# A four-mixer network on one core: the first pair of an attention block projected without the norm's row factor

## The chip, the cores and the metric

One core of a Trainium2 chip runs the whole program. The metric is the device time of one execution in microseconds (us), lower is better. TensorE (PE) multiplies, PEld is its weight load, VectorE (DVE) and ScalarE (ACT) work elementwise, GpSimd (POOL) and the SyncE queue (SP) do the rest. The three runs shown of the kernel before have a median of 911.96 us.

## The reference

Four layers follow one another on a sequence of 256 positions with 1024 features: a gated delta rule mixer, an attention block ("the middle block" here, the reference's `moba_mixer`; with 256 positions it is plain causal attention within one block), a norm, a retention mixer and a chunked attention mixer. What matters for the change is the middle block's entry:

```python
def rms_norm(x, g):
    xf = x.astype(jnp.float32)
    y = xf * lax.rsqrt(jnp.mean(xf * xf, axis=-1, keepdims=True) + EPS)
    return (y * g.astype(jnp.float32)).astype(x.dtype)
...
    kv = rms_norm(x, kv_norm_g) @ w_kv
...
    x = x + moba_mixer(rms_norm(x, b_norm_g[j]), b_w_in[j], b_w_out[j], kb, vb, k_mean, rel_bias)
...
    proj = hn @ w_in
    q = proj[..., :B_W].reshape(bsz, s, B_HEADS, B_DH)
    z = proj[..., B_W:]
    o = moba_attention(q, kb, vb, k_mean, rel_bias)
    return (o * jax.nn.silu(z)).astype(hn.dtype) @ w_out
```

The factor `rsqrt(mean(x*x))` is one number for each position. It can be multiplied to x before the product with `w_in` or to the product's result.

## The kernel before

Everything is kept transposed: features on the 128 partitions, positions on the free axis. x is 8 tiles of 128 x 256. Each product is a "job" of 1024 x 256 weights: 8 tiles k, two output halves, and three matmuls for each, as every fp32 operand is split into a high part (rounded to fp32r) and a low part, and high-high, high-low and low-high are summed. So a job is 48 matmuls of 128 x 128 by 256 columns. Jobs alternate between two PSUM banks; `bank_free` counts when a bank's reader is done.

Weights stream in chunks of 1 MB, one for a job in this part of the program. SP issues chunk c after DVE has split chunk c - 3 (line 342). A chunk is split in two halves ("units"): ACT writes the high part `whi` (`high`, line 854, the instruction on line 863), DVE the low part `wlo` (`low`, line 1218, line 1234). Four units of each are held, and the high part of a unit waits for TensorE to be done with the unit four before it. Job J's chunk is J; in `attend` the engines split chunk J + 1 under the name of job J (`split_c` on ACT, `lows` on DVE).

Each engine's order is written out by hand, and it is strict. The part around the change:

- Jobs 16 to 19 (`JOB_OUT_A`) project the first mixer's output. DVE's `add_x` (line 1462) adds each job's bank to two tiles of x (line 1473); ACT's `square_x` (line 895) squares them (line 904).
- `x_sums(1)` (line 776): 8 fp32 products with ones sum the squares over the partitions. ACT's `rsqrt` (Ln on line 882, Exp on line 884) makes the row factor of it, after an explicit load of its function table (line 852) and the split of chunk 21.
- DVE multiplies x by the row factor into `hf` (line 1549, four instructions). ACT makes high parts of `hf` times the gain for two operands (line 1145): `b_norm` into `ohi` tiles 8 to 15, then `kv_norm` into `hhi`. DVE makes the low parts (`lo_of`, line 1546).
- The middle block (`attend`, jobs 20 to 35): four pairs of heads, each with four jobs, q (J), z (J + 1), k (J + 2) and v (J + 3). q and z read the b_norm operand, k and v the kv_norm operand. For pair i the scores (fp32 products of `qn` and `kn`) come behind job J + 3, `turn(i)`, the transposes of the softmax on line 733, behind job J + 5, and `mix(i)` behind J + 6. ACT copies q, k and v out of PSUM and applies Silu to z.
- Beside this, DVE sums the conditioning matrices ("ADA", `pair_sums`, lines 1312 to 1319): pair n is summed behind the split of chunk `ADA_AT[n]`, the ring for the next one is loaded by SP three chunks later, and TensorE's `ada` follows job `ADA_AT[n]`.

Of the kernel before, what the change touches and what calls it, by code (L numbers as in the profile page):

```python
# [18 lines left out]
KT = D // P  # L19
# [3 lines left out]
F32 = mybir.dt.float32  # L23
# [36 lines left out]
    return [JOB_OUT_D + 4 + 2 * (job - JOB_OUT_D) + h for h in range(2)]  # L60


ADA_AT = [10, 11, 12, 13, 14, 15, 23, 26, 29, 32, 35, 43, 46, 48, 51, 53, 56, 58, 61, 63, 78, 82, 86, 90]


def laid_at(c):
# [8 lines left out]
def two_blocks(nc, x_in, wts, ada_w, cols_in, const_in, lmask_in, w_ab, rel_b, rel_d, dtab, pos, out,  # L75
               scr_b, scr_d):
    ctx = ExitStack()
    with ctx:
# [172 lines left out]
        rs_ok_sem = sem("rs_ok")  # L251
        hf_ok_sem = sem("hf_ok")
        hh_ok_sem = sem("hh_ok")
        h_ok_sem = sem("h_ok")
        dve_own_sem = sem("dve_own")
        ab_ok_sem = sem("ab_ok")
# [182 lines left out]
        def _(pe):  # L439
# [9 lines left out]
                else:  # L449
                    pe.wait_ge(bank_free[J % 2], max(J // 2 - 6, 0))  # L450

            def job(J, form, hi, lo, ready=None, split=None, at={}, heads=2):

                bank = v2(pj[J % 2])
                bank_empty(J)
                cs = chunks_of(J)
                for n, c in enumerate(cs):
                    for half in range(2):
                        unit = 2 * c + half
                        pe.wait_ge(lo_ok_sem, unit + 1)  # L460
                        for kk in range(4):
                            k = 4 * half + kk
                            kx = 8 * n + k
                            if kx in at:
                                at[kx]()
                            if split is not None and kx % heads == 0:
                                pe.wait_ge(o_split_sem, split + kx // heads + 1)
                            if ready is not None and n == 0:
                                pe.wait_ge(h_ok_sem, ready + k + 1)
                            for t in range(2):  # L470
                                w = slice(t * P, t * P + P)
                                for a, (ws, hs) in enumerate(((whi, hi), (whi, lo), (wlo, hi))):
                                    first = n == 0 and k == 0 and t == 0 and a == 0
                                    last = n == len(cs) - 1 and k == KT - 1 and a == 2
                                    if form == "T":
                                        m = mm(bank[:, t, :], ws[:, unit % UNITS, kk, w], hs[:, kx, :], first, last)
                                    else:
                                        m = mm(bank[:, t, :], hs[:, kx, w], ws[:, unit % UNITS, kk, :], first, last)
                        m.then_inc(w_units_sem, 1)
# [242 lines left out]
            def attend(J0, pairs, soft0, o0, h_q, h_kv, normed, ready, extra):  # L722
# [28 lines left out]
                for i in range(pairs):  # L751
                    J = J0 + 4 * i
                    h_1, h_2 = (h_kv, h_q) if normed else (h_q, h_kv)
                    job(J, "T", *h_q, ready=ready[0] if i == 0 else None)
                    extra(J)
                    job(J + 1, "T", *h_1)
                    extra(J + 1)
                    if i:
                        turn(i - 1)
                    if normed:  # L760
                        sums(lambda t: sqb[:, 0:2, :], 1, 512, qk_sq_sem, lambda t: 4 + 2 * i + 1)
                    job(J + 2, "T", *h_2, ready=ready[1] if i == 0 and not normed else None)
                    extra(J + 2)
                    if i:
                        mix(i - 1)
                    if normed:
                        sums(lambda t: sqb[:, 2:4, :], 1, 512, qk_sq_sem, lambda t: 4 + 2 * i + 2)
                    job(J + 3, "S", *h_kv)
                    extra(J + 3)
                    if normed:  # L770
                        scores(i, soft0, lambda: pe.wait_ge(qk_ok_sem, 2 * i + 2))
                    else:
                        scores(i, soft0, lambda: banks_copied(J))
                return lambda: turn(pairs - 1), lambda: mix(pairs - 1)

            x_sums(1)

            turn_last, mix_last = attend(JOB_B, 4, 0, 4, (ohi[:, 8:16, :], olo[:, 8:16, :]), (hhi, hlo), False, (8, 16), ada_after)
            for J in range(JOB_OUT_B, JOB_C):
                if J == JOB_OUT_B:  # L780
                    job(J, "T", ohi, olo, split=4, at={4: turn_last, 6: mix_last})
# [53 lines left out]
                ada_after(J)  # L835
            x_sums(3)

            turn_last, mix_last = attend(JOB_D, 8, 4, 12, (hhi, hlo), (hhi, hlo), True, (32, 32), ada_after)
            for J in range(JOB_OUT_D, N_JOBS):
                if J == JOB_OUT_D:  # L840
                    job(J, "T", ohi, olo, split=12, at={8: turn_last, 12: mix_last})
# [5 lines left out]
        def _(act):  # L847
# [47 lines left out]
            def square_x(J0, gain=None):  # L895

                for n in range(4):
                    J = J0 + n
                    for c in chunks_of(J):
                        if n or c > chunks_of(J0)[0] or J0 == JOB_OUT_A:  # L900
                            high(c + 1)
                    bank_taken(act, J)
                    if gain is None:
                        act.activation(xsq[:, 2 * n:2 * n + 2, :], x[:, 2 * n:2 * n + 2, :], ACT.Square).then_inc(sq_ok_sem, 1)
                    else:
                        for t in (2 * n, 2 * n + 1):
                            m = act.activation(xsq[:, t, :], x[:, t, :], ACT.Square, scale=gain(t))
                        m.then_inc(sq_ok_sem, 1)
# [153 lines left out]
            def attend(J0, pairs, soft0, v0, normed):  # L1062
# [18 lines left out]
                for i in range(pairs):  # L1081
# [4 lines left out]
                    if i:  # L1086
                        if normed:
                            ln_exp_set()
                        soft(i - 1)
                    if not normed:  # L1090
                        act.wait_ge(w_units_sem, 2 * chunks_of(J)[-1] + 2)
                        act.wait_ge(s_ok_sem, 2 * (soft0 + i))
                        act.activation(qn[:, :, :], bank(J), ACT.Copy).then_inc(bank_free[J % 2], 1)
                        if i:
                            split_c(J + 1)
                        act.wait_ge(w_units_sem, 2 * chunks_of(J + 1)[-1] + 2)
                        act.activation(zs[:, 2 * (i % 2):2 * (i % 2) + 2, :], bank(J + 1), ACT.Silu).then_inc(bank_free[(J + 1) % 2], 1)
                        if i == 2:
                            act.wait_ge(fin_rope_sem, 2)
                            act.activation(sint, tr1, ACT.Sin)  # L1100
                            act.activation(cost, tr2, ACT.Sin).then_inc(fin_rope_sem, 1)
                        if i:
                            turned(i - 1)
                        split_c(J + 2)
                        split_c(J + 3)
                        act.wait_ge(w_units_sem, 2 * chunks_of(J + 2)[-1] + 2)
                        act.activation(kn[:, :, :], bank(J + 2), ACT.Copy).then_inc(bank_free[J % 2], 1)
                        act.wait_ge(w_units_sem, 2 * chunks_of(J + 3)[-1] + 2)
                        act.wait_ge(o_ok_sem, v0 + i)
                        act.activation(vs[:, :, 0:256], bank(J + 3), ACT.Copy).then_inc(bank_free[(J + 3) % 2], 1)  # L1110
                        continue
# [27 lines left out]
            ln_exp_set()  # L1139
            high(JOB_B + 1)  # L1140
            rsqrt(rsb[:, 0, :], S, 1.0 / D)
            for dst, gain in ((ohi[:, 8:16, :], "b_norm"), (hhi, "kv_norm")):
                for t in range(KT):
                    act.wait_ge(hf_ok_sem, 8 + t // 2 + 1)
                    act.activation(dst[:, t, :], hf[:, t, :], ACT.Copy, scale=col(gain, t)).then_inc(hh_ok_sem, 1)
            high(JOB_B + 2)
            attend(JOB_B, 4, 0, 4, False)

# [59 lines left out]
        def _(dve):  # L1208
# [253 lines left out]
            def add_x(J0, gate=None, before_last=None):  # L1462

                for n in range(4):
# [6 lines left out]
                    sums_done(J)  # L1471
                    if gate is None:
                        dve.tensor_tensor(x[:, 2 * n:2 * n + 2, :], bank(J), x[:, 2 * n:2 * n + 2, :], ALU.add).then_inc(bank_free[J % 2], 1)
                    else:
                        for t in range(2):
                            k = 2 * n + t
# [3 lines left out]
            def attend(J0, pairs, soft0, bias, normed):  # L1480
# [31 lines left out]
                for i in range(pairs):  # L1512
# [6 lines left out]
                        scale_p(i - 1)  # L1519
                    if normed or i:  # L1520
                        lows(J + 1)
                    lows(J + 2)
                    if normed:
                        next_rs()
                        dve.wait_ge(s_ok_sem, 2 * (soft0 + i))
# [17 lines left out]
            def lo_of(prep, t, gain, hi, lo):  # L1543

                dve.wait_ge(hh_ok_sem, 8 * prep + t + 1)
                dve.scalar_tensor_tensor(out=lo[:, t, :], in0=hf[:, t, :], scalar=col(gain, t), in1=hi[:, t, :].bitcast(F32), op0=ALU.mult, op1=ALU.subtract).then_inc(h_ok_sem, 1)

            for n in range(4):
                dve.tensor_tensor(hf[:, 2 * n:2 * n + 2, :], x[:, 2 * n:2 * n + 2, :], wide(rsb[:, 0, :], 2), ALU.mult).then_inc(hf_ok_sem, 1)
                if n:  # L1550
                    for t in (2 * n - 2, 2 * n - 1):
                        lo_of(1, t, "b_norm", ohi[:, 8:16, :], olo[:, 8:16, :])
            for t in (6, 7):
                lo_of(1, t, "b_norm", ohi[:, 8:16, :], olo[:, 8:16, :])
            for t in range(KT):
                lo_of(2, t, "kv_norm", hhi, hlo)
            low(JOB_B + 2)
            dve.wait_ge(bias_ok_sem, 128)
            attend(JOB_B, 4, 0, A(bias_at, 8, 384), False)
            def scaled_gain(l):  # L1560
# [211 lines left out]
```

## Time and profile before

| | |
|---|---|
| median of the three runs | 911.96 us (909.32 to 914.17) |
| the profiled execution | 909.5 us, span 907.6 us |
| mean granted clock of TensorE | 0.981 |
| TensorE matmul busy | 858.5 us, 95% |
| DVE busy | 580.2 us, 64% |
| ACT busy | 481.2 us, 53% |
| jobs 16 to 19 | about 210 to 236 us |
| middle block and its output projection | about 244 to 382 us |

Times in all rows are from the start of the span. The last add of jobs 16 to 19 is at 236 us. A matmul's row is its own duration, which overlaps with the next one's; the spacing of two starts is what one costs in a stream. The granted clock is 1.00 at 2.4 GHz and 0.50 at 1.2 GHz. A merged row carries a count (x16).

### The profile page before, as it was taken

How to read it: one execution, taken by the hardware profiler on the slowest of the kernel's cores; microseconds unless marked ns; L12 is line 12 of the kernel's file. 1: busy time of each engine (PE TensorE's matmuls, PEld its weight loads, DVE VectorE, ACT ScalarE, POOL GpSimd, SP SyncE). 2: the span in 40 equal slices, each digit the busy share in tenths (PEclk: the TensorE clock that was granted, in tenths of full speed). 3: DMA queues.
4: the chain of work that ended last, by engine and by line, in shares of the span. 5: the costliest groups of instructions: out<-in, count | busy, mean ns of one | idle time of the engine just before them, and what ended most of it. 6: DMA issues, size and time to landing. Idle time of an engine off the chain costs nothing.

```text
span 907.6 us, 16161 instructions
## 1 busy us (share of the span) xinstructions
PE 858.5 (95%) x6742; PEld 830.6 (92%) x6742; DVE 580.2 (64%) x1025; ACT 481.2 (53%) x740; POOL 33.5 (4%) x57
## 2 busy tenths in 40 slices
PE   5999999999899998989979998898999999999998
PEld 4899999998799998989979998798999999999998
DVE  4886875637657667477766786446476666656652
ACT  5754554345655654555443433345676576666741
POOL 2100500002000000000000000200000000000000
PEclk9999999999899999999999999899999999999999
DMA  6463654333746465426646464496354464434350
GB/s 264 147 217 109 108 186 148 134 99 93 244 175 219 165 232 187 139 94 229 236 139 215 157 235 182 124 257 223 140 197 172 148 224 143 147 133 153 129 207 24
DMA packets 26487, 153.69 MB, mean 169 GB/s; under 512 B 2848, under 2 KB 3376, under 8 KB 12080
## 3 DMA queue, kind: packets, MB, share of 16 engines
q1 hardware_dynamic: 24432, 146.37, 46.7%
q0 software_dynamic: 1984, 6.31, 3.8%
q8 instruction: 53, 0.87, 0.4%
q14 instruction: 18, 0.15, 0.1%
HBM read 150.04 MB, written 2.62 MB: 168 GB/s over the span
## 4 chain that ended last, share of the span: by engine, by line
PE 86%; DVE 9%; ACT 3%; issue 1%; DMA 1%; SPq 0%; DVEq 0%; ACTq 0%
PE ps L443 83%; DVE wlo L1234 2%; PE ps L637 1%; DVE olo L1279 1%; ACT whi L863 1%; PE ps L733 1%; ACT L852 1%; DVE arena L1594 1%; DVE arena L1590 1%; DMA raw<-weights 1%; DVE ohi L1277 1%; DVE ada_ring L1315 0%; DVE arena L1301 0%; ACT arena L882 0%; DVE early L1266 0%
## 5 line engine op out<-in xcount | busy, mean ns | idle before, releaser
L1234 DVE TENSOR_TENSOR wlo<-raw,whi 128x1024 fp32r<-128x1024 f32 x224 | 265.3, 1222 | 176.9 <-ACT whi L863 176.9
L443 PE MATMUL ps<-hhi,whi 128*128 128x256 f32 x960 | 280.7, 292 | 18.5 <-DVE wlo L1234 7.9
L443 PE MATMUL ps<-hlo,whi 128*128 128x256 f32 x960 | 273.4, 285 | 0.0
L443 PE MATMUL ps<-hhi,wlo 128*128 128x256 f32 x960 | 273.3, 285 | 0.0
L863 ACT ACTIVATE whi<-raw 128x1024 fp32r<-128x1024 f32 x224 | 225.9, 1052 | 82.8 <-PE ps L443 61.2
L443 PEld LDWEIGHTS ps<-hhi,whi 128*128 128x128 f32 x960 | 185.8, 194 | 22.9 <-issue 22.1
L443 PEld LDWEIGHTS ps<-hlo,whi 128*128 128x128 f32 x960 | 186.0, 194 | 2.0 <-issue 1.9
L443 PEld LDWEIGHTS ps<-hhi,wlo 128*128 128x128 f32 x960 | 185.8, 194 | 0.0
L443 PE MATMUL ps<-ohi,whi 128*128 128x256 f32 x512 | 149.8, 293 | 12.5 <-DVE olo L1279 7.9
L443 PE MATMUL ps<-olo,whi 128*128 128x256 f32 x512 | 147.5, 288 | 0.0
L443 PE MATMUL ps<-ohi,wlo 128*128 128x256 f32 x512 | 147.3, 288 | 0.0
L443 PEld LDWEIGHTS ps<-ohi,whi 128*128 128x128 f32 x512 | 101.0, 197 | 14.0 <-issue 9.9
L443 PE MATMUL ps<-arena 128*128 128x128 f32 (+2 forms) x656 | 101.0, 302 | 3.0 <-DVE olo L1279 3.0
L443 PEld LDWEIGHTS ps<-arena 128*128 128x128 f32 x656 | 92.2, 195 | 10.0 <-issue 5.5
L443 PEld LDWEIGHTS ps<-olo,whi 128*128 128x128 f32 x512 | 101.0, 197 | 0.3 <-issue 0.2
L443 PEld LDWEIGHTS ps<-ohi,wlo 128*128 128x128 f32 x512 | 100.8, 197 | 0.0
L443 PE MATMUL ps<-whi,hhi 128*128 128x256 f32 x320 | 94.2, 294 | 0.0
L443 PE MATMUL ps<-wlo,hhi 128*128 128x256 f32 x320 | 90.5, 283 | 0.0
L443 PE MATMUL ps<-whi,hlo 128*128 128x256 f32 x320 | 90.5, 283 | 0.0
L443 PEld LDWEIGHTS ps<-whi,hhi 128*128 128x128 f32 x320 | 61.4, 192 | 1.9 <-issue 1.9
L443 PEld LDWEIGHTS ps<-whi,hlo 128*128 128x128 f32 x320 | 61.3, 192 | 1.9 <-issue 1.9
L443 PEld LDWEIGHTS ps<-wlo,hhi 128*128 128x128 f32 x320 | 61.3, 192 | 0.0
(194 smaller groups left out, 867.6 us busy)
## 6 DMA issues: line engine op xcount, KB each, us to landing
raw<-weights SPq DMA_DIRECT2D x112, 1024.0 KB, 5.0
ada_ring<-ada SPq DMA_DIRECT2D x24, 1024.0 KB, 5.1
arena<-bias_rows_d POOLq DMA_DIRECT2D x4, 512.0 KB, 14.1
x<-x_t SPq DMA_DIRECT2D x2, 512.0 KB, 4.5
bias_rows_d<-early POOLq DMA_DIRECT2D x1, 1024.0 KB, 12.4
arena<-bias_rows_b POOLq DMA_DIRECT2D x4, 256.0 KB, 7.3
arena<-bias_rows_d POOLq DMA_DIRECT2D x4, 256.0 KB, 16.2
out_t<-x SPq DMA_DIRECT2D x4, 256.0 KB, 2.2
```

Source lines behind the costliest of these rows:

```text
L443: return pe.matmul(o, l, r, start=start, stop=stop, skip_group_check=skip)
L637: m = pe.transpose(b[:, m4 * P:m4 * P + P], tt[:, 4 * g + m4, :], ident)
L733: m = pe.transpose(turned_bank(hh, soft0)[:, a * P:a * P + P], ts[:, hh, c0:c0 + P], ident)
L852: act.add_instruction(mybir.InstLoadActFuncSet(name=nc.get_next_instruction_name(), act_func_set_id=6, ins=[], outs=[]))
L863: act.activation(whi[:, unit % UNITS, :, :], raw[:, c % RAW, 4 * half:4 * half + 4, :], ACT.Copy).then_inc(hi_ok_sem, 1)
L1234: dve.tensor_tensor(wlo[:, unit % UNITS, :, :], raw[:, c % RAW, 4 * half:4 * half + 4, :], whi[:, unit % UNITS, :, :].bitcast(F32), ALU.su ...
L1277: own(dve.tensor_copy(ohi[:, r, :], src))
L1279: return dve.tensor_tensor(olo[:, r, :], src, ohi[:, r, :].bitcast(F32), ALU.subtract)
L1590: own(dve.tensor_tensor(of[:, :, :], v2(ps[3 + b]), wide(rsb[:, 0, :], 2), ALU.mult))
L1594: own(dve.scalar_tensor_tensor(out=of[:, t, :], in0=of[:, t, :], scalar=col("ret_gn", 4 * h + k), in1=zs_c[:, 4 * (h % 2) + k, :], op0=ALU ...
```

## The change

For the first pair alone, q and z (jobs 20 and 21) are projected from x times the gain, without the row factor, and DVE multiplies both results by the row factor when it takes them out of PSUM. In detail:

- While jobs 16 to 19 run, ACT makes the high parts of x times `b_norm` into `hhi` (8 instructions, ahead of each square), and DVE the low parts into `hlo` (8, one job behind, the last four behind the last add). TensorE waits for these low parts on `xg_lo_sem`.
- `x_sums(1)` moves from ahead of job 20 to between its k = 3 and k = 4.
- After the row factor, DVE and ACT make the `kv_norm` operand, now into `ohi`/`olo` tiles 8 to 15, and only later, behind the splits of chunk 23, the `b_norm` operand for pairs 1 to 3, now into `hhi`/`hlo`.
- DVE's order becomes: `hf` and kv low parts 0 to 5, q of job 20 times the factor (instead of ACT's copy), first half of chunk 22, kv low parts 6 and 7, second half, z of job 21 times the factor, chunk 23, eight low parts of `b_norm`. ACT applies Silu to the scaled z in place.
- Four ADA places move: 23, 26, 29, 32 become 25, 28, 30, 33.

```diff
-ADA_AT = [10, 11, 12, 13, 14, 15, 23, 26, 29, 32, 35, ...
+ADA_AT = [10, 11, 12, 13, 14, 15, 25, 28, 30, 33, 35, ...
...
+                    elif i == 0:
+                        job(J, "T", *h_q, ready=0, ready_sem=xg_lo_sem, at={4: lambda: x_sums(1)})
+                    else:
+                        job(J, "T", *h_q, ready=16 if i == 1 else None)
...
-            x_sums(1)
...
                     bank_taken(act, J)
+                    if J0 == JOB_OUT_A:
+                        for t in (2 * n, 2 * n + 1):
+                            act.activation(hhi[:, t, :], x[:, t, :], ACT.Copy, scale=col("b_norm", t)).then_inc(xg_hi_sem, 1)
...
-                    if not normed:
+                    if not normed and i == 0:
+                        act.wait_ge(z0_scaled_sem, 1)
+                        act.activation(zs[:, 0:2, :], zs[:, 0:2, :], ACT.Silu).then_inc(bank_free[(J + 1) % 2], 1)
+                        split_c(J + 2)
+                        for t in range(KT):
+                            act.activation(hhi[:, t, :], hf[:, t, :], ACT.Copy, scale=col("b_norm", t)).then_inc(hh_ok_sem, 1)
+                        split_c(J + 3)
+                    elif not normed:
...
+                        if J0 == JOB_OUT_A:
+                            for m in (n - 1, n) if n == 3 else (n - 1,):
+                                for t in range(2 * m, 2 * m + 2) if m >= 0 else ():
+                                    dve.wait_ge(xg_hi_sem, t + 1)
+                                    dve.wait_ge(bank_free[(JOB_OUT_A + m) % 2], (JOB_OUT_A + m) // 2 - 5)
+                                    dve.scalar_tensor_tensor(out=hlo[:, t, :], in0=x[:, t, :], scalar=col("b_norm", t), in1=hhi[:, t, :].bitcast(F32), op0=ALU.mult, op1=ALU.subtract).then_inc(xg_lo_sem, 1)
...
+            sums_done(JOB_B)
+            dve.tensor_tensor(qn[:, :, :], bank(JOB_B), wide(rsb[:, 0, :], 2), ALU.mult).then_inc(bank_free[JOB_B % 2], 1)
+            low(JOB_B + 2, range(1))
+            kv_lo(6)
+            kv_lo(7)
+            low(JOB_B + 2, range(1, 2))
+            sums_done(JOB_B + 1)
+            dve.tensor_tensor(zs[:, 0:2, :], bank(JOB_B + 1), wide(rsb[:, 0, :], 2), ALU.mult).then_inc(z0_scaled_sem, 1)
+            dve.wait_ge(z0_scaled_sem, 1)
+            low(JOB_B + 3)
             for t in range(KT):
-                lo_of(2, t, "kv_norm", hhi, hlo)
-            low(JOB_B + 2)
+                lo_of(2, t, "b_norm", hhi, hlo)
```

## Rows read from the trace of the kernel before

**Rows 1.** The page, section 1: busy time, share, instructions by engine.

```profile
PE 858.5 (95%) x6742; PEld 830.6 (92%) x6742; DVE 580.2 (64%) x1025; ACT 481.2 (53%) x740; POOL 33.5 (4%) x57
```

**Rows 2.** TensorE's waits, 251 to 382 us: total us, times, longest.

```profile
PE ps L443 <- DVE olo L1279: 2.0, 1, 2.0
PE ps L733 <- issue: 0.7, 1, 0.7
```

**Rows 3.** Chain of waits, 234 to 260 us: start, us, what.

```profile
236.22 0.70 DVE x L1473
...
237.59 1.28 ACT L852
...
238.89 1.06 ACT whi L863
...
239.98 2.36 DVE wlo L1234 x2
```

**Rows 4.** Timeline of TensorE, 235 to 260 us: start, us, instruction, [idle before <-releaser].

```profile
236.02 3.62 PE L443 MATMUL ps<-arena,ones 128*128 128x256 f32 x16
244.15 0.55 PE L443 MATMUL ps<-ohi,whi 128*128 128x256 f32 x1 [4.51 <-DVE olo L1546]
...
250.05 0.36 PE L443 MATMUL ps<-ohi,whi 128*128 128x256 f32 x1
...
258.40 0.28 PE L443 MATMUL ps<-hhi,whi 128*128 128x256 f32 x1
258.52 0.28 PE L443 MATMUL ps<-hlo,whi 128*128 128x256 f32 x1
```

**Rows 5.** TensorE by stretch (busy, PEclk, DMA share, GB/s) and in the timeline.

```profile
244.00:250.00 6.00, 5.85 (x27) 0.50 0.39 153
...
362.00:368.00 6.00, 6.00 (x40) 0.72 0.12 51
...
521.00:527.00 6.00, 6.00 (x51) 1.00 0.70 201
...
361.54 0.39 PE L443 MATMUL ps<-ohi,whi 128*128 128x256 f32 x1 [1.97 <-DVE olo L1279]
...
520.36 0.35 PE L443 MATMUL ps<-hhi,whi 128*128 128x256 f32 x1 [1.94 <-DVE wlo L1234]
```

**Rows 6.** Timeline of ACT, 236 to 260 us.

```profile
236.95 0.63 ACT L904 ACTIVATE arena<-x 128x512 f32<-128x512 f32 x1 [3.23 <-DVE x L1473]
...
240.80 0.45 ACT L882 ACTIVATE arena<-ps,epsc 128x256 f32<-128x256 f32 x1
...
246.43 0.91 ACT L1145 ACTIVATE ohi<-arena,columns 128x256 fp32r<-128x256 f32 x2 [0.49 <-DVE arena L1549]
...
254.45 1.28 ACT L1097 ACT_TABLE_LOAD   x1
258.60 0.60 ACT L1097 ACTIVATE arena<-ps 128x512 f32<-128x512 f32 x1 [2.87 <-PE ps L443]
```

**Rows 7.** Timeline of DVE, 232 to 253 us; line 1590 by form (busy, mean ns).

```profile
232.80 2.36 DVE L1234 TENSOR_TENSOR wlo<-raw,whi 128x1024 fp32r<-128x1024 f32 x2 [1.58 <-ACT whi L863]
...
242.25 1.29 DVE L1549 TENSOR_TENSOR arena<-x,arena 128x512 f32<-128x512 f32 x2
...
246.31 1.67 DVE L1546 SCALAR_TENSOR_TENSOR olo<-arena,columns,ohi 128x256 fp32r<-128x256 f32 x4
...
251.52 1.23 DVE L1234 TENSOR_TENSOR wlo<-raw,whi 128x1024 fp32r<-128x1024 f32 x1 [0.37 <-ACT whi L863]
...
L1590 DVE TENSOR_TENSOR arena<-ps,arena 128x512 f32<-128x512 f32 x5 | 3.4, 686 | 0.1
```

**Rows 8.** The page, section 6: DMA issues, count, KB each, us to landing.

```profile
ada_ring<-ada SPq DMA_DIRECT2D x24, 1024.0 KB, 5.1
```

**Rows 9.** DVE's timeline and the chain of waits near chunk 30's split.

```profile
309.36 2.36 DVE L1234 TENSOR_TENSOR wlo<-raw,whi 128x1024 fp32r<-128x1024 f32 x2 [0.68 <-ACT whi L863]
...
310.41 0.71 PE ps L733 x6
```

More of the change, by code:

```diff
@@ L60, in chunks_of @@
     return [JOB_OUT_D + 4 + 2 * (job - JOB_OUT_D) + h for h in range(2)]
-ADA_AT = [10, 11, 12, 13, 14, 15, 23, 26, 29, 32, 35, 43, 46, 48, 51, 53, 56, 58, 61, 63, 78, 82, 86, 90]
+ADA_AT = [10, 11, 12, 13, 14, 15, 25, 28, 30, 33, 35, 43, 46, 48, 51, 53, 56, 58, 61, 63, 78, 82, 86, 90]
 def laid_at(c):
@@ L253, in two_blocks @@
         hh_ok_sem = sem("hh_ok")
+        xg_hi_sem = sem("xg_hi")
+        xg_lo_sem = sem("xg_lo")
+        z0_scaled_sem = sem("z0_scaled")
         h_ok_sem = sem("h_ok")
@@ L450, in bank_empty, with job @@
                     pe.wait_ge(bank_free[J % 2], max(J // 2 - 6, 0))
-            def job(J, form, hi, lo, ready=None, split=None, at={}, heads=2):
+            def job(J, form, hi, lo, ready=None, split=None, at={}, heads=2, ready_sem=h_ok_sem):
                 bank = v2(pj[J % 2])
@@ L468, in job @@
                             if ready is not None and n == 0:
-                                pe.wait_ge(h_ok_sem, ready + k + 1)
+                                pe.wait_ge(ready_sem, ready + k + 1)
                             for t in range(2):
@@ L753, in attend @@
                     h_1, h_2 = (h_kv, h_q) if normed else (h_q, h_kv)
-                    job(J, "T", *h_q, ready=ready[0] if i == 0 else None)
+                    if normed:
+                        job(J, "T", *h_q, ready=ready if i == 0 else None)
+                    elif i == 0:
+                        job(J, "T", *h_q, ready=0, ready_sem=xg_lo_sem, at={4: lambda: x_sums(1)})
+                    else:
+                        job(J, "T", *h_q, ready=16 if i == 1 else None)
                     extra(J)
@@ L761, in attend @@
                         sums(lambda t: sqb[:, 0:2, :], 1, 512, qk_sq_sem, lambda t: 4 + 2 * i + 1)
-                    job(J + 2, "T", *h_2, ready=ready[1] if i == 0 and not normed else None)
+                    job(J + 2, "T", *h_2, ready=ready if i == 0 and not normed else None)
                     extra(J + 2)
@@ L774, in attend @@
                 return lambda: turn(pairs - 1), lambda: mix(pairs - 1)
-            x_sums(1)
-            turn_last, mix_last = attend(JOB_B, 4, 0, 4, (ohi[:, 8:16, :], olo[:, 8:16, :]), (hhi, hlo), False, (8, 16), ada_after)
+            turn_last, mix_last = attend(JOB_B, 4, 0, 4, (hhi, hlo), (ohi[:, 8:16, :], olo[:, 8:16, :]), False, 8, ada_after)
             for J in range(JOB_OUT_B, JOB_C):
@@ L836, in _ @@
             x_sums(3)
-            turn_last, mix_last = attend(JOB_D, 8, 4, 12, (hhi, hlo), (hhi, hlo), True, (32, 32), ada_after)
+            turn_last, mix_last = attend(JOB_D, 8, 4, 12, (hhi, hlo), (hhi, hlo), True, 32, ada_after)
             for J in range(JOB_OUT_D, N_JOBS):
@@ L1093, in attend @@
                         act.activation(qn[:, :, :], bank(J), ACT.Copy).then_inc(bank_free[J % 2], 1)
-                        if i:
-                            split_c(J + 1)
+                        split_c(J + 1)
                         act.wait_ge(w_units_sem, 2 * chunks_of(J + 1)[-1] + 2)
@@ L1101, in attend @@
                             act.activation(cost, tr2, ACT.Sin).then_inc(fin_rope_sem, 1)
-                        if i:
-                            turned(i - 1)
+                        turned(i - 1)
                         split_c(J + 2)
                         split_c(J + 3)
+                    if not normed:
                         act.wait_ge(w_units_sem, 2 * chunks_of(J + 2)[-1] + 2)
@@ L1141, in _ @@
             rsqrt(rsb[:, 0, :], S, 1.0 / D)
[L1142 to L1145, printed above, removed]
+            for t in range(KT):
+                act.wait_ge(hf_ok_sem, 8 + t // 2 + 1)
+                act.activation(ohi[:, 8 + t, :], hf[:, t, :], ACT.Copy, scale=col("kv_norm", t)).then_inc(hh_ok_sem, 1)
             high(JOB_B + 2)
@@ L1521, in attend @@
                         lows(J + 1)
-                    lows(J + 2)
+                        lows(J + 2)
                     if normed:
@@ L1546, in lo_of @@
                 dve.scalar_tensor_tensor(out=lo[:, t, :], in0=hf[:, t, :], scalar=col(gain, t), in1=hi[:, t, :].bitcast(F32), op0=ALU.mult, op1=ALU.subtract).then_inc(h_ok_sem, 1)
+            kv_lo = lambda t: lo_of(1, t, "kv_norm", ohi[:, 8:16, :], olo[:, 8:16, :])
             for n in range(4):
@@ L1550, in _ @@
                 if n:
[L1551 to L1554, printed above, removed]
+                    kv_lo(2 * n - 2)
+                    kv_lo(2 * n - 1)
+            sums_done(JOB_B)
[8 more added lines that the diff above has]
+            low(JOB_B + 3)
             for t in range(KT):
-                lo_of(2, t, "kv_norm", hhi, hlo)
-            low(JOB_B + 2)
+                lo_of(2, t, "b_norm", hhi, hlo)
             dve.wait_ge(bias_ok_sem, 128)
```

## The prediction

> **What bounds the kernel now.** I read the page first: TensorE is busy 858.5 of 907.6 us, DVE and ACT far less [rows 1]. So time can only be won where TensorE stands still or runs at half its clock. The table of waits for the middle attention block says where that is not the case: from 251 us to 382 us TensorE waits for 2.7 us in all, for two causes [rows 2]. Whatever is won ahead of 251 us is therefore handed on, if the block is still fed in time.
>
> The chain of waits around the seam between the output projection (jobs 16 to 19) and the block (jobs 20 on) shows what is won there [rows 3]. The last add to x starts at 236.22, a table load at 237.59 (1.28 us), the split of chunk 21 on ACT at 238.89 and on DVE at 239.98 (2.36 us) and then the products with the row factor; job 20 starts at 244.15 [rows 4], released by a low part of b_norm's. TensorE's own list shows the same from its side [rows 4]: the sums of squares (8 fp32 products, 16 records) run from 236.02 for 3.62 us; then nothing for 4.51 us; then job 20 at 244.15, and job 22, the first to read the kv operand, at 258.40. Jobs 20 and 21 are 96 matmuls. They take 258.40 - 244.15 = 14.25 us; at the spacing of the full clock, 258.52 - 258.40 = 0.12 us, they would take 11.52. The missing 2.73 us lie in the first 28: they need 250.05 - 244.15 = 5.90 us, 0.21 each, and the granted clock from 244 to 250 is 0.50, that is 1.2 GHz, after TensorE had stood idle [rows 5].
>
> **The change part by part.**
>
> The old stretch from the start of the sums to the start of job 22 is 258.40 - 236.02 = 22.38 us [rows 4]. The new one holds half of job 20 (k 0 to 3, 24 matmuls, 2.88 us), the sums, the other half, and job 21. For the sums I take 3.5 us: 16 spacings of about 0.215, or with the drain 3.62 [rows 4]. If nothing waits: 2.88 + 3.5 + 2.88 + 5.76 = 15.0 us. The difference is 7.4 us: the idle 4.5, the half clock 2.7, and 0.2 of latency at the first matmul. Job 20 no longer needs the row factor, so what it does need must be ready by 236.0.
>
> Start of job 20: its operand is x times the gain, high part by ACT, low part by DVE. Tiles 0 to 3 are made beside jobs 17 to 19 and are long ready. Tiles 6 and 7 follow the last add, which ends at 236.9: ACT makes the high parts at about 0.45 each (2 in 0.91) [rows 6], DVE the four outstanding low parts at 0.42 each (4 in 1.67) [rows 7], done by 238.6. TensorE wants tile 4 only after the sums, at 242.4. Cover: nearly 4 us. The squares move 0.9 us later behind two high parts: 236.95 + 0.9 + 0.63 = 238.5. The sums start at 238.9 and take the last squares as their last two products. Cover again.
>
> Work added while jobs 16 to 19 run: 8 ACT instructions (3.6 us) and 8 DVE instructions (3.4 us). The high parts stand ahead of the splits of chunks 18 to 20, which move back by 0.9 us. Of chunk 20, DVE's low part started at 232.80 [rows 7]; now at 233.7, its first half done at 234.9, and job 20 wants it at 236.0. Chunks 18 and 19 have the same order and about the same spare time of 1 us. I cost it at nothing; without that cover it is 0.9 us once.
>
> The row factor: the sums now end at about 242.5 instead of 239.6. But ACT first splits chunk 21, from 239.8 (squares 238.5 plus the 1.28 table load) to 241.8; before, this pushed the Ln to 240.80 [rows 6]. Now Ln starts at 242.55, Exp ends at 243.45, and DVE starts the product x times the factor at 243.5 instead of 242.25 [rows 7], only 1.25 later.
>
> Then a queue on DVE decides. From the rows of before, shifted by 1.25: the four products and six low parts of the kv operand end at 248.4 (before, numbers 4 to 7 started at 246.31, four in 1.67 [rows 7]); q times the factor out of PSUM, 0.69 as the product of the same shape on line 1590 [rows 7], ends at 249.1; the split of chunk 22 waits for ACT (its eight kv high parts end at 248.6: before, the last two of the first operand started at 246.43 and took 0.91 [rows 6]; the first half of the chunk's high part follows at 249.6) and ends its first half at 250.8, at 1.23 a half [rows 7]. Job 22 wants it at 251.0. Slack 0.2. Two low parts and the second half end at 252.8, wanted at 253.9. Then z times the factor ends at 253.5, Silu at 254.1, the high part of chunk 23 at 255.1 and 256.1, its low part at 256.3 and 257.5; job 23 wants it at 256.8 and 259.7. Slack 0.5. The wait for job 21's end (251.0) in front of z's product costs nothing, as DVE comes there at 252.8. Behind that product are queued chunk 23's split and the eight low parts of b_norm; for these wait pair 1's jobs.
>
> The eight high and low parts of b_norm: ACT 256.0 to 259.3, DVE 257.5 to 260.8, then chunk 24 till 262.1 and 263.3. Job 24 starts at 262.6 plus the scores, 263.9. Slack 1.8. The keys' copy behind them on ACT ends at 262.0, wanted at 262.6. Nothing on the path, if the above holds.
>
> The q copy of ACT for the first pair goes (0.6), DVE gets two products (1.4). All that nets out away from TensorE.
>
> The moved ADA places (23, 26, 29, 32 to 25, 28, 30, 33): 8 DVE instructions and a sum, 3.5 us each, the same number; the ring's DMA is still issued three chunks later behind them on SP's queue, and at 5.1 us to landing [rows 8] the shortest distance, two chunks from 28 to 30, gives it over 10. What matters is that the sum of chunk 25 now stands in front of pair 0's scores. Before, chunk 29's stood so in front of pair 1's: there chunk 30's low part starts at 309.36, its first half ends at 310.6, and TensorE turned pair 1 at 310.41 for 0.71 us [rows 9] and went on without a wait [rows 2]. Slack 0.5. The same pattern now comes at chunk 25 and 33. I take it at 0.
>
> Sum: -7.4, with 0 for the feeds, whose bound is 0 to 1.5. Bound below: nothing here can win more than 7.4 except a luckier clock later.
>
> One rule weighed. The load of Silu's table stands in the trace right behind the q copy, at 254.45, while the Silu itself starts at 258.60 [rows 6]: it runs ahead of the wait. In the change it would then run at 250.5 to 251.8, ahead of the wait for z's product at 253.5, and cost nothing; behind the wait it would put 1.28 us into the link with slack 0.5, so 0.8 on the path. The Trainium skill (ScalarE: Activation LUTs, "What ACT_TABLE_LOAD costs") gives a switch 2.66 us, a drain being half of it. By it the load would still just fit ahead of the wait, and behind it cost an estimated 2.2. The rows show no such drain: the load at 237.59 takes 1.28 and the next ACT instruction starts at 238.89 [rows 3].
>
> **The rivals.**
>
> A, fed late: the slacks of 0.2 and 0.5 (and 0.5 at chunk 26) are smaller than what I can read from shifted rows. If each slips, TensorE waits 0.5 to 1 us at jobs 22, 23 or 26, 1.5 in all: gain 5.9, time 906.1. For it: everything passes through one DVE queue. Against: each term has a measured row.
>
> B, the clock takes it back later: TensorE's half-clock stretches behind later waits don't follow from the length of the wait alone. After 1.97 us of idle, at 361.54, the granted clock is 0.72 for six us; after 1.94 us, at 520.36, it is 1.00 [rows 5]. All later work moves by 7.4 us, so each stretch can come out otherwise, 1.7 us apiece at 0.72 (six us times 0.28). Two more such: +3.4, time 908.0. Two fewer: 901.2. The three times of before, 909.3 to 914.2, spread as much. The Trainium skill (TensorE: Matmul & The Clock Gate, "What's actually happening") says that the activity monitor's window is free-running and not tied to the kernel's start, which fits these two rows.
>
> C, slower: the ADA sums of 3.5 us stand in front of the scores at chunks 25 and 33, and their slack of 0.5 turns negative. Then TensorE waits for the softmax and for chunks 26 and 34, up to 3.5 us at each place, and falls to half clock, 2.7 each: 12.4 - 7.4 = +5.0, time 917.0. It decides from the point where chunk 26's first low half ends after pair 0's turn. Against it: the precedent of chunk 29 [rows 9].
>
> D, the change doesn't do what it says: job 20 still waits, say for the low parts of x, or the sums for the squares. The cover is 4 us; to lose it all, job 20 would have to wait for the table load and chunk 21 as before. Then only extra work is left: 912.
>
> **How the numbers follow.** The profiled execution took 909.5 us for a span of 907.6; less 7.4 that is 902.1 and 900.2. It is at the low end of the three runs shown, whose median is 911.96, so the forecast for the median is 911.96 - 7.4 = 904.6. Chances: the forecast 0.57, A 0.20, B 0.17 (half to each side), C 0.02, D 0.04. The range takes in A, B and the spread of the runs: 901 to 909. A measurement of this kernel can tell about 0.5% from no change, which is 4.6 us. Faster by more than that needs a gain above 4.6: the forecast 0.57, nearly all of A 0.19, half of B 0.09, together 0.85. Within it: D, the rest of B and A, 0.13. Slower: C, 0.02.
>
> **What would show it.** Right: between 236 and 262 us no idle row of TensorE above 0.5, a granted clock of 1.00 there, the sums' 16 records between two halves of job 20 near 239, job 22 at about 251.0, scores of pair 0 at about 262.6. Job 22 or 23 with idle time released by DVE's wlo is A. Half-clock stretches other than before behind 355 us are B. A wait at about 276 us is C. A first product of x and the row factor later than 244 would make the whole link late and the forecast wrong by that much.

## The result

The changed kernel takes 904.64 us (904.05 to 905.05, five runs) against 910.57 for the kernel before on the same chip (909.32 to 914.17, five runs). The medians differ by 5.9 us, 0.65%. The ratio of the runs on record is 0.9923, 95% interval 0.9907 to 0.9940: 0.8% faster, which is 5.5 to 8.5 us. Forecast were 904.6 us and a gain of 7.4, and both agree with this. The profiled execution of the changed kernel took 904.05 us, span 902.2; that of before 909.5 and 907.6.

The same work as in [rows 4], on TensorE's timeline of the changed kernel (line 446 is line 443 of before):

```profile
238.38 0.28 PE L446 MATMUL ps<-hhi,whi 128*128 128x256 f32 x1
...
241.26 3.61 PE L446 MATMUL ps<-arena,ones 128*128 128x256 f32 x16
244.52 0.47 PE L446 MATMUL ps<-hhi,whi 128*128 128x256 f32 x1
...
253.34 0.29 PE L446 MATMUL ps<-ohi,whi 128*128 128x256 f32 x1
```

Job 20 starts at 238.38, directly behind job 19, with tile 0 of x times the gain. Its first half ends at 241.26, the sums run for 3.61 us between the halves, and job 22, the first reader of the kv operand (now `ohi`), starts at 253.34. From the end of job 19 to job 22 it is 14.96 us; it was 22.38. The idle row of 4.51 us is gone, and by stretch the clock is whole:

```profile
238.00:244.00 6.00, 6.00 (x42) 5.69 (x41) 3.46 (x7) 4.67 (x6) 0.00 (x0) 1.00 0.81 325
244.00:250.00 6.00, 6.00 (x50) 5.90 (x49) 5.63 (x11) 3.57 (x9) 0.00 (x0) 1.00 0.53 179
250.00:256.00 6.00, 6.00 (x53) 6.00 (x52) 5.17 (x9) 4.35 (x6) 0.00 (x0) 1.00 0.01 4
```

(columns: stretch, us, then busy time and count of PE, PEld, DVE, ACT, POOL, granted clock, DMA share, GB/s). TensorE is busy all 18 us at a granted clock of 1.00, which is 2.4 GHz; before, 244 to 250 showed 0.50 [rows 5].

DVE's queue, which [rows 7] was the source for:

```profile
245.87 1.29 DVE L1570 TENSOR_TENSOR arena<-x,arena 128x512 f32<-128x512 f32 x2 [0.37 <-ACT arena L890]
...
250.74 0.68 DVE L1575 TENSOR_TENSOR arena<-ps,arena 128x512 f32<-128x512 f32 x1
251.95 1.23 DVE L1248 TENSOR_TENSOR wlo<-raw,whi 128x1024 fp32r<-128x1024 f32 x1 [0.53 <-ACT whi L869]
...
255.02 0.68 DVE L1581 TENSOR_TENSOR arena<-ps,arena 128x512 f32<-128x512 f32 x1
257.42 2.36 DVE L1248 TENSOR_TENSOR wlo<-raw,whi 128x1024 fp32r<-128x1024 f32 x2 [1.72 <-ACT whi L869]
259.70 3.26 DVE L1566 SCALAR_TENSOR_TENSOR hlo<-arena,columns,hhi 128x256 fp32r<-128x256 f32 x8
```

The first half of chunk 22's low part ends at 251.95 + 1.23 = 253.18, and job 22 reads it at 253.34: a slack of 0.16 us. (Where job 22 did wait for this half, in e4 and e8 below, it started 0.10 us after the end of the half, so some 0.06 us of it was to spare.) The row of 251.95 tells one thing more: DVE had stood idle 0.53 us for ACT's high part. And on ACT the table for Silu is loaded ahead of the wait for z:

```profile
252.89 1.28 ACT L1101 ACT_TABLE_LOAD   x1
255.74 0.63 ACT L1101 ACTIVATE arena<-arena 128x512 f32<-128x512 f32 x1 [1.57 <-DVE arena L1581]
```

But the whole stretch lies 2.36 us later in the span than before, although all work up to job 16 is the same. So I cut each profiled execution into three: up to the last add to x (its start), from there to the first pair's transposes (`turn(0)`), and the rest of the span. The add and the turn of the changed kernel:

```profile
238.58 0.69 DVE L1487 TENSOR_TENSOR x<-ps,x 128x512 f32<-128x512 f32 x1 [0.26 <-PE ps L446]
...
278.03 0.85 PE L736 MATMUL ps<-cst,arena 128*128 128x128 f32 x6
```

The names e1 to e8 are those of the experiments below; the last three columns are lengths in us.

| profiled execution | last add at | add to turn | rest | span |
|---|---|---|---|---|
| before | 236.22 | 46.96 | 624.4 | 907.6 |
| before once more (e7) | 236.50 | 46.96 | 624.4 | 907.9 |
| before with idle products in the wait (e2) | 239.03 | 44.31 | 623.1 | 906.4 |
| changed | 238.58 | 39.45 | 624.2 | 902.2 |
| changed once more (e6) | 240.04 | 39.46 | 628.5 | 908.0 |
| changed, sums ahead of job 20 (e3) | 238.42 | 39.46 | 624.3 | 902.2 |
| changed, ADA places back (e1) | 236.22 | 40.55 | 624.1 | 900.9 |
| changed, two products more (e4) | 238.85 | 40.03 | 627.3 | 906.2 |
| changed, four products more (e8) | 238.46 | 41.22 | 625.6 | 905.3 |
| changed, idle products in seven later waits (e5) | 236.52 | 39.46 | 616.1 | 892.1 |

The middle column is what the change acts on. It repeats to 0.01 us and falls from 46.96 to 39.45, by 7.51 us. The other two hold little of the change, and move by up to 4 us. Ahead of the last add stand the first products of x and the gain; TensorE's last wait ahead of it ends at 216.78 in the kernel before and at 219.13 in the changed one, 19.44 and 19.45 us ahead of the add, so they cost nothing. Behind the first turn stand three of the moved ADA places.

### The profile page after: what moved, and what is told of

Read it like the earlier page. It is cut to its first block, busy times and chain, and to the rows that moved or that the text cites. A ratio compares the mean times of both kernels' runs of the same rounds, so it can differ in the third digit from the quotient of the medians.

```text
span 902.2 us, 16186 instructions
## 1 busy us (share of the span) xinstructions
PE 857.1 (95%) x6742; PEld 828.9 (92%) x6742; DVE 584.0 (65%) x1035; ACT 483.5 (54%) x747; POOL 33.5 (4%) x57
## 4 chain that ended last, share of the span: by engine, by line
PE 86%; DVE 8%; ACT 3%; issue 1%; DMA 1%; SPq 0%; DVEq 0%; ACTq 0%
PE ps L446 84%; DVE wlo L1248 2%; PE ps L640 1%; DVE olo L1293 1%; PE ps L736 1%; ACT whi L869 1%; DVE arena L1622 1%; ACT L858 1%; DVE arena L1618 1%; DMA raw<-weights 1%; DVE ohi L1291 1%; DVE ada_ring L1329 0%; DVE arena L1315 0%; ACT arena L888 0%; DVE early L1280 0%
## 5 line engine op out<-in xcount | busy, mean ns | idle before, releaser
L446 PE MATMUL ps<-hhi,whi 128*128 128x256 f32 x1024 | 299.1, 292 | 18.8 <-DVE wlo L1248 7.9
L446 PE MATMUL ps<-hlo,whi 128*128 128x256 f32 x1024 | 291.2, 284 | 0.0
L446 PE MATMUL ps<-ohi,whi 128*128 128x256 f32 x448 | 130.2, 291 | 7.9 <-DVE olo L1293 7.9
L446 PE MATMUL ps<-olo,whi 128*128 128x256 f32 x448 | 128.2, 286 | 0.0
L446 PE MATMUL ps<-ohi,wlo 128*128 128x256 f32 x448 | 128.0, 286 | 0.0
L446 PE MATMUL ps<-whi,hhi 128*128 128x256 f32 x256 | 75.8, 296 | 0.0
L446 PE MATMUL ps<-wlo,hhi 128*128 128x256 f32 x256 | 72.4, 283 | 0.0
L446 PE MATMUL ps<-whi,hlo 128*128 128x256 f32 x256 | 72.4, 283 | 0.0
L1329 DVE SCALAR_TENSOR_TENSOR ada_ring<-ada_ring,sil 128x256 f32<-128x256 f32 x144 | 60.1, 488 | 0.0
L446 PE MATMUL ps<-arena,ones 128*128 128x256 f32 (+1 forms) x132 | 43.6, 461 | 8.5 <-DVE arena L1298 8.5
```

Of the source, the lines that this page charges most:

```text
L446: return pe.matmul(o, l, r, start=start, stop=stop, skip_group_check=skip)
L1329: own(dve.scalar_tensor_tensor(out=b, in0=b, scalar=sil[:, k:k + 1], in1=ring[:, :, k - 2, :], op0=ALU.mult, op1=ALU.add))
```

## The experiments

**What each part of the gain is.** e2 leaves the wait of before and takes only the half clock away:

```diff
             x_sums(1)
+            for _ in range(19):
+                mm(ps[3][:, :], ident_r[:, :], causal_r[:, :].unsqueeze(1).to_broadcast([P, 4, P]), True, True)
```

> The kernel before, with 19 products of 512 columns into an unused PSUM bank behind the sums of squares, whose results nobody reads; they fill the 4.5 us in which TensorE stands idle. It takes the half clock away and leaves the wait. My theory (the gain of 7.4 us is 4.7 of wait and 2.7 of half clock): granted clock 1.00 from 244 to 250 us, job 20 starts when it did, job 22 comes 2.7 us earlier, time 910.6 - 2.7 = 907.9. Rival: the clock falls for another reason (the change of operand, the cold stretch is due to the phase): still a stretch at 0.50, time 910 to 911.

Measured 908.99 us against 910.73 (12 and 23 runs), ratio 0.9984, 0.9968 to 1.0000. TensorE's timeline:

```profile
238.83 3.61 PE L443 MATMUL ps<-arena,ones 128*128 128x256 f32 x16
242.09 4.68 PE L443 MATMUL ps<-causal_r,ident_r 128*128 128x512 f32 x19
246.97 0.36 PE L443 MATMUL ps<-ohi,whi 128*128 128x256 f32 x1 [0.19 <-DVE olo L1548]
```

and the stretch behind it:

```profile
246.80:252.80 6.00, 5.83 (x49) 5.87 (x50) 6.00 (x16) 5.17 (x13) 0.00 (x0) 1.00 0.40 160
```

Job 20 starts 246.97 - 238.83 = 8.14 us behind the start of the sums, as before (244.15 - 236.02 = 8.13 [rows 4]): the wait is untouched. The clock behind it is 1.00, and the part from add to turn is 44.31 instead of 46.96, 2.65 us less. So of the 7.5 us, 2.7 are the half clock; what is left, 4.9, is the wait with its latency, by difference. The rival, that the clock would fall for another reason than the wait, is out for this place. The whole time fell by 1.7 and not by 2.7, to 908.99 and not to the 907.9 expected; the interval reaches to no change at all, so the time cannot carry the verdict. The stretch can.

**Whether the sums had to go inside job 20.** e3:

```diff
-                        job(J, "T", *h_q, ready=0, ready_sem=xg_lo_sem, at={4: lambda: x_sums(1)})
+                        job(J, "T", *h_q, ready=0, ready_sem=xg_lo_sem)
...
+            x_sums(1)
             turn_last, mix_last = attend(JOB_B, 4, 0, 4, (hhi, hlo), ...
```

> The changed kernel with the sums of squares ahead of job 20 again instead of between its halves. My theory: six of the eight sums need only older squares and take 2.6 us, by which time the last squares are just ready, so TensorE waits 0.0 to 0.3 us; the row factor comes 2.9 us earlier less ScalarE's split of chunk 21, which delays it; the stretch from job 19's end to job 22 stays 15.0 to 15.3 us and the time is 904.6 to 904.9. Rival: the place inside job 20 is what hides the squares and the table load; without it TensorE waits 1 us or more, 905.6 or later.

Measured 904.81 us (6 runs), ratio 0.9926 (0.9905 to 0.9946), the same as the changed kernel. Its timelines of TensorE and DVE:

```profile
238.22 3.61 PE L446 MATMUL ps<-arena,ones 128*128 128x256 f32 x16
241.48 0.47 PE L446 MATMUL ps<-hhi,whi 128*128 128x256 f32 x1
...
253.18 0.28 PE L446 MATMUL ps<-ohi,whi 128*128 128x256 f32 x1
```

```profile
242.97 2.36 DVE L1249 TENSOR_TENSOR wlo<-raw,whi 128x1024 fp32r<-128x1024 f32 x2 [2.29 <-ACT whi L870]
245.25 1.29 DVE L1571 TENSOR_TENSOR arena<-x,arena 128x512 f32<-128x512 f32 x2
...
251.32 1.23 DVE L1249 TENSOR_TENSOR wlo<-raw,whi 128x1024 fp32r<-128x1024 f32 x1 [0.53 <-ACT whi L870]
```

The stretch to job 22 is 253.18 - 238.22 = 14.96 us, the same to the hundredth. The sums run without a gap, so the last squares were in time. The place of the sums carries nothing of the gain. What it changes is slack: chunk 22's first half is now ready at 252.55, 0.63 us ahead of job 22 instead of 0.16. It is not the 2.9 us that the sums moved, as DVE is at chunk 21 until 245.3 whatever the row factor does.

**The slack at job 22.** e4 puts two more products ahead of q's on DVE, e8 four:

```diff
+            for to in (of, kn):
+                dve.tensor_tensor(to[:, :, :], bank(JOB_B), wide(rsb[:, 0, :], 2), ALU.mult)
             dve.tensor_tensor(qn[:, :, :], bank(JOB_B), wide(rsb[:, 0, :], 2), ALU.mult).then_inc(bank_free[JOB_B % 2], 1)
```

> The changed kernel with two more products of 0.69 us on VectorE ahead of q's (their results are not used), 1.4 us in the queue in front of chunk 22. My theory (the feed of job 22 has a slack of 0.2 us): job 22 starts 1.2 us late, released by wlo, the rest moves with it, time 905.8. Rival (VectorE has room, busy 65%): job 22 starts where it did, 904.6.

Measured 904.95 us (902.26 to 908.05, 6 runs), ratio 0.9929 (0.9904 to 0.9954): in the time nothing can be told. From add to turn it is 40.03, that is +0.58, about half of what I expected and not the rival's nothing. DVE and TensorE:

```profile
251.00 1.29 DVE L1576 TENSOR_TENSOR arena<-ps,arena 128x512 f32<-128x512 f32 x2
252.20 0.69 DVE L1577 TENSOR_TENSOR arena<-ps,arena 128x512 f32<-128x512 f32 x1
252.80 1.22 DVE L1248 TENSOR_TENSOR wlo<-raw,whi 128x1024 fp32r<-128x1024 f32 x1
```

```profile
254.12 0.36 PE L446 MATMUL ps<-ohi,whi 128*128 128x256 f32 x1 [0.35 <-issue]
```

The chunk's row has lost its idle time before it. Its half ends at 252.80 + 1.22 = 254.02, and job 22 starts at 254.12; the trace names no engine as its releaser ("issue"), the two times do. I had counted the slack on TensorE's side and left out that DVE itself was waiting for ACT there (249.1 against 249.6 in my own working). By the starts of the rows, two more products put q's back by 252.20 - 251.00 = 1.20 us; 0.53 were idle, 0.16 slack, and 0.51 is left to show, against 0.58 measured. With four this makes a forecast that can fail:

> The changed kernel with four more products of 0.69 us on VectorE ahead of q's instead of two (results unused). With two, job 22 came 0.6 us late and not 1.2: VectorE had stood idle 0.5 us for ScalarE's high part of chunk 22, and 0.2 us was slack. If that is so, two more cost their whole 1.3 us: from the last add to the first turn 39.45 + 0.6 + 1.3 = 41.3 to 41.4 us. Rival: TensorE makes it up later by shorter waits, as with two: 40.0 to 40.6.

Measured 41.22 us from add to turn, 1.19 more than with two, and an idle row of 1.53 ahead of job 22 (DVE first, then TensorE):

```profile
250.61 2.48 DVE L1576 TENSOR_TENSOR arena<-ps,arena 128x512 f32<-128x512 f32 x4
253.01 0.68 DVE L1577 TENSOR_TENSOR arena<-ps,arena 128x512 f32<-128x512 f32 x1
```

```profile
254.92 0.36 PE L446 MATMUL ps<-ohi,whi 128*128 128x256 f32 x1 [1.53 <-issue]
```

The one run took 907.23 us. Four products put q's back by 253.01 - 250.61 = 2.40 us; less 0.69 that is 1.71, and 1.77 was measured (41.22 - 39.45). The last two alone cost 1.20 us of DVE and made the stretch 1.19 us longer. Beyond the first 0.7 us, each us put ahead of chunk 22 on DVE is a us of the stretch, and the rival, that TensorE makes it up later, is out. DVE's busy share of 65% says nothing here.

**What the moved ADA places do.** e1 puts them back:

```diff
-ADA_AT = [10, 11, 12, 13, 14, 15, 25, 28, 30, 33, 35, ...
+ADA_AT = [10, 11, 12, 13, 14, 15, 23, 26, 29, 32, 35, ...
```

> The changed kernel with the four ADA places back at 23, 26, 29, 32. My theory: the sum of 3.5 us behind chunk 23 then stands on VectorE ahead of the eight low parts of b_norm and of chunk 24, whose first half would be ready about 1.4 us after job 24 could start. TensorE waits there for wlo or hlo, 1.0 to 1.5 us, and the time is 905.7 to 906.1 against 904.6 for the changed kernel. Rival: the sums find room anywhere, since VectorE is busy 65% of the span: no wait at job 24, 904.2 to 905.0.

Measured 907.3 us (902.75 to 911.45, 12 runs), ratio 0.9965, 0.9946 to 0.9984. DVE and TensorE:

```profile
257.86 2.46 DVE L1329 SCALAR_TENSOR_TENSOR ada_ring<-ada_ring,sil 128x256 f32<-128x256 f32 x6
260.36 0.43 DVE L1333 TENSOR_TENSOR ada_sum<-ada_ring 128x256 f32<-128x256 f32 x1
260.70 3.25 DVE L1566 SCALAR_TENSOR_TENSOR hlo<-arena,columns,hhi 128x256 fp32r<-128x256 f32 x8
263.87 4.62 DVE L1248 TENSOR_TENSOR wlo<-raw,whi 128x1024 fp32r<-128x1024 f32 x4
```

```profile
265.18 0.35 PE L446 MATMUL ps<-hhi,whi 128*128 128x256 f32 x1 [0.77 <-issue]
```

Job 24 waits 0.77 us for chunk 24 behind the sum, and the part from add to turn is 1.10 longer, as expected of the mechanism. The time was expected at 905.7 to 906.1 and missed that: the median of 907.3 is 2.5 us above that of e3, measured beside it, which is more than the mechanism. Whether the rest is the clock or something else, the one profiled execution can't say: it was the shortest of the twelve. So the moved places are part of the gain, 1.1 us of it shown.

**What the time outside the stretch hangs on.** Two kernels once more:

> The changed kernel once more, to pair with the next and to see whether the last add to x ahead of job 20 falls at 236.2 or at 238.4 to 239.0 us, where traces of kernels with the same work until then differ. If that is the state of the clock early in the program and not the change, it can fall at either; from the last add to the first turn 39.4 to 39.5 us in any case; time 904 to 905.5.

> The kernel before once more. From the last add to x to the first turn it took 47.0 us, of which 2.7 hang on a stretch at half clock. If that stretch can come out shorter, it is 45 to 47 us here; the last add at 236.2 or 238.4 to 239.0 us; time 909 to 912.

e6: 904.76 us (902.07 to 909.86, 6 runs), ratio 0.9945 (0.9923 to 0.9966); e7: 909.80 in one run. From add to turn 39.46 and 46.96: both repeat, and the half clock at job 20 did not come out shorter in e7. The last add fell at 240.04 and at 236.50; the former is later than either value that I had named. The granted clock of 72 to 78 us, where the two programs do the same, in e7 and in e6:

```profile
72.00:78.00 6.00, 6.00 (x45) 5.48 (x45) 2.60 (x7) 3.44 (x9) 0.00 (x0) 1.00 0.54 178
```

```profile
72.00:78.00 6.00, 6.00 (x27) 5.12 (x27) 2.60 (x7) 3.44 (x10) 0.00 (x0) 0.64 0.51 178
```

TensorE is busy all six us in both, yet in e6 the clock is 0.64, and 27 matmuls are started instead of 45. In the changed kernel's first profile it is 0.72, in before's 1.00. That is the larger part of the 2.4 us by which the stretch lies later: the job behind these six us starts at 78.67 against 76.32, and 0.75 us of the 2.35 was there before (the 8 narrow products ahead of it start at 71.57 against 70.82). It is not the only place: in e3 the granted clock is 1.00 here, and its 2.2 us were there by 48.51 us, where the kernel before is at 46.30. Nor is it tied to the change: e2, with the old order, has 0.75 here.

The part behind the stretch moved too. In e6 the rest is 4.3 us longer than in the first profile of the same kernel. One of the places is a wait that is the same 3.14 us in both; the first profile, row and stretch behind it, then e6's:

```profile
625.16 0.35 PE L446 MATMUL ps<-hhi,whi 128*128 128x256 f32 x1 [3.14 <-DVE hlo L1276]
...
626.00:632.00 6.00, 6.00 (x49) 5.86 (x49) 4.25 (x11) 3.01 (x6) 0.00 (x0) 1.00 0.31 130
```

```profile
629.88 0.41 PE L446 MATMUL ps<-hhi,whi 128*128 128x256 f32 x1 [3.14 <-DVE hlo L1276]
...
630.00:636.00 6.00, 6.00 (x39) 6.00 (x40) 4.97 (x13) 3.06 (x6) 0.00 (x0) 0.72 0.39 156
```

The same program after the same wait had the full clock in one execution and 0.72 in the other.

**A version that is faster than both.** In e5, the changed kernel gets idle products in seven later waits:

```diff
-                    job(J, "T", ohi, olo, split=4, at={4: turn_last, 6: mix_last})
+                    job(J, "T", ohi, olo, split=4, at={4: turn_last, 6: lambda: (mix_last(), fill(7, ps[3]))})
...
             x_sums(2)
+            fill(19, ps[6])
...
                 J = JOB_C + 6 * h
+                fill((0, 0, 23, 7)[h], ps[6])
...
+            fill(12, ps[6])
             mix_c(3)
...
-                    job(J, "T", ohi, olo, split=8, at={8: lambda: sums_c(3)}, heads=4)
+                    job(J, "T", ohi, olo, split=8, at={8: lambda: (sums_c(3), fill(16, ps[6]))}, heads=4)
...
             x_sums(3)
+            fill(12, ps[6])
```

> The changed kernel with idle products of 512 columns (results unused) in seven later waits of TensorE: 7 behind the last mix of the middle block, 19 behind x_sums(2), 23 and 7 ahead of the retention jobs 52 and 58, 12 ahead of the last retention mix, 16 behind its sums, 12 behind x_sums(3). Each fill ends some 0.4 us before the wait does, so no wait is shortened. In the changed kernel's trace the stretches at half clock behind these waits cost about 10 us (windows from 356 to 584 us). My theory: the clock stays up, the gaps' ends stay where they are, 904.6 - 8 to 10 = 895 to 897. Rival: the clock falls by its own phase anyway, as it did from 74 to 78 us with TensorE busy, and part of the fills delays jobs: 901 to 905.

Measured 896.89 us (893.97 to 897.5, 4 runs) against 910.38, ratio 0.9854, 0.9840 to 0.9869. Behind the waits the changed kernel showed these stretches:

```profile
356.00:362.00 6.00, 5.58 (x34) 5.58 (x35) 1.75 (x3) 2.58 (x4) 0.00 (x0) 0.72 0.26 108
384.00:390.00 6.00, 5.08 (x31) 5.11 (x32) 5.64 (x15) 4.04 (x9) 0.00 (x0) 0.72 0.53 175
...
559.00:565.00 6.00, 5.41 (x17) 4.72 (x18) 2.71 (x3) 0.00 (x0) 0.00 (x0) 0.50 0.37 119
```

and about the same places in e5, which lie 2 to 7 us earlier:

```profile
354.00:360.00 6.00, 5.65 (x48) 5.63 (x48) 2.29 (x4) 2.81 (x4) 0.00 (x0) 1.00 0.24 100
381.00:387.00 6.00, 5.74 (x45) 5.52 (x45) 5.47 (x14) 4.05 (x9) 0.00 (x0) 1.00 0.40 157
...
552.00:558.00 6.00, 5.85 (x37) 5.04 (x37) 3.80 (x6) 1.34 (x3) 0.00 (x0) 1.00 0.26 69
```

The rest behind the first turn is 616.1 us instead of 624.2. The waits are all still there, now filled, and the mean granted clock of the profiled execution is 0.998 instead of 0.985. 7.9 us lie between the medians of e5 and of the changed kernel on the same chip (904.76, e6), more than the change itself brought.

## Why the prediction was right, and where it was not

**The stretch.** Forecast 15.0 us from job 19's end to job 22, measured 14.96. The gain of 7.4 was 4.5 of wait, 2.7 of half clock and 0.2 of latency; e2 gives 2.65 for the half clock alone. This was the step that carried the sum, and it held. (The first 28 matmuls take 250.25 - 244.15 = 6.10 us and not the 5.90 of the working, which runs to the start of the 28th; the 2.73 us are right with 6.10.)

**The feeds.** My times for DVE and ACT up to b_norm's low parts, moved by 2.36 us, stand in the trace to within 0.2: first product with the row factor 243.5 (245.87 - 2.36 = 243.51), q's product from 248.4 (248.38), chunk 22's first half ready at 250.8 (250.82), Silu at 253.5 (253.38), b_norm's low parts from 257.5 (257.34). Chunk 24's came up to 0.4 earlier than worked out. The slack of 0.2 at job 22 was 0.16. Rival A did not come about, but e4 and e8 show how near it was, and that its price beyond DVE's 0.53 us of idle time and the slack is a us for a us.

**The table load.** It ran ahead of the wait, from 252.89, as [rows 6] had it in the kernel before. Of the drain that the Trainium skill (ScalarE: Activation LUTs, "What ACT_TABLE_LOAD costs") counts with a switch, the traces show nothing: in [rows 3] the next ACT instruction starts 0.02 us after the load's end, and the load itself starts 0.01 us after the end of the square ahead of it (236.95 + 0.63 = 237.58 [rows 6], 237.59 [rows 3]). Here the 1.57 us of idle time between load and Silu would have hidden it in any case.

**The ADA places.** I costed the new ones at nothing, by the precedent of chunk 29, and that held: TensorE has no idle row from the start of job 20 to 350.88 us, well past the second turn. But I looked only at whether the new places do harm. e1 shows that without the move the change would have lost 1.1 us at job 24, so leaving them would have been a cost that my working had no line for.

**The latter part of the sum.** 7.5 us in the stretch became 5.9 in the medians. The interval of the comparison itself, 5.5 to 8.5 us, holds the 7.4; that of e6, 3.1 to 7.0 us, doesn't, so part of the gain is likely lost outside the stretch, some 1.5 us by the medians. That is the term that I took as zero in the forecast and held as rival B: the clock outside the stretch. In the profiled pair the accounts close: 7.51 less 2.36 ahead of the stretch, plus 0.2 in the rest, is 5.4, the difference of the spans. B was looked for behind the stretch only, at waits. In this pair the loss came ahead of it, where TensorE was busy and the work was the same; in e6 it came behind it as well, 4.3 us in the rest, at waits as B has it. Kernels with the old order had the last add at 236.2, 236.5 and 239.0, kernels with the new one at 236.2, 236.5 and five times at 238.4 or later; the rest was 623.1 to 624.4 us with the old order, and 624.1 to 628.5 with the new one and no fills behind it. Whether the change makes the late case more frequent, or ten profiles are too few, stays open.

That the median came within 0.1 us of the forecast of 904.6 is luck: the median of before, from which I subtracted, was 1.2 to 1.6 us higher (911.96) than in each later comparison (910.57, 910.73, 910.38), and that made up for the 1.5 us.

**C and D.** Neither came about: no wait at chunk 26 (C), and job 20 started directly behind job 19 (D).

## What to carry to other kernels

A factor that belongs to a column of the result can be moved behind the product, and then the product can start while the factor is still being made; what it is worth is read from one place, the idle row and the stretch at half clock behind it. Compare the part that the change acts on, which repeated to 0.01 us here, and not whole times alone, when the other parts move by 2 to 4. And where a wait of TensorE can't be taken away, idle products in it keep the clock: filled in seven waits they brought 7.9 us here.

## What the runs showed of the hardware

The granted clock fell to half while TensorE had no idle row (none between 47 and 79 us). Two-us stretches of the changed kernel:

```profile
72.00:74.00 2.00, 2.00 (x12) 1.00 0.62 156
74.00:76.00 2.00, 2.00 (x9) 0.50 0.87 369
76.00:78.00 2.00, 2.00 (x14) 0.64 0.03 8
```

(PE only; columns as above). Just ahead of it TensorE worked on narrow products:

```profile
71.57 0.95 PE L446 MATMUL ps<-ones,early 128*128 128x1 f32 x8
72.45 2.28 PE L446 MATMUL ps<-r,cst 16*128 16x256 f32 x8
```

The kernel before issued the same at 70.82 and stayed at 1.00, so these products alone don't decide it; of the ten profiles five are below 1.00 from 72 to 78 us and five are not. Nor does the length of a wait decide: behind 3.14 us of idle at 625.16 the changed kernel had 1.00, behind 1.97 us at 356.42 it had 0.72, and behind the same 3.14 us in e6 it had 0.72. That fits what the Trainium skill (TensorE: Matmul & The Clock Gate, "What's actually happening") says of a monitor that runs on its own time. In the ten profiles the last add ahead of the stretch came at 236.2 to 236.5 us or 2 to 4 us later, with not one instruction ahead of the first output job changed.
